# Delta rule: the decay's running sums spread from stored rows, by 16-row selector products in two row groups and two banks, two tiles at a time

## The reference, cut to what matters

```
g_cum = jnp.cumsum(g, axis=2)
diff = g_h[..., :, None] - g_h[..., None, :]
decay = jnp.where(incl, jnp.exp(jnp.where(incl, diff, 0.0)), 0.0)
l_strict = jnp.where(strict, jnp.einsum('bnthd,bnshd->bnhts', k_beta, k) * decay, 0.0)
t_inv = lax.linalg.triangular_solve(eye + l_strict, ...)
att = jnp.where(incl, jnp.einsum('bnthd,bnshd->bnhts', q, k) * decay, 0.0)
```

## Time and profile before

| | before |
|---|---|
| three runs, us | 2592.38, 2593.41, 2596.2 (median 2593.41) |
| the profiled execution's own time, us | 2584.35 |
| its span, us | 2582.4 |
| TensorE busy, us | 2280.8 (88%) |
| DVE, ACT, POOL busy, us | 965.1, 804.1, 350.5 |
| mean granted clock of TensorE | 0.934 of full speed |

### The profile page before, as it was taken

One profiled execution on the slowest core, in us unless ns is written; L12 is line 12 of the kernel. 1 busy time (PEld: TensorE's weight loads), 2 busy tenths in 40 slices (PEclk: granted clock), 3 DMA queues, 4 the chain that ended last, 5 costly groups with the idle time before them and its releaser, 6 DMA issues. The chain is left out here.

```text
span 2582.4 us, 32117 instructions
## 1 busy us (share of the span) xinstructions
PE 2280.8 (88%) x11226; PEld 1516.3 (59%) x11226; DVE 965.1 (37%) x2407; ACT 804.1 (31%) x2147; POOL 350.5 (14%) x568
## 2 busy tenths in 40 slices
PE   5999988698988878999999999989588886899998
PEld 3676555454554666555574437766375555766677
DVE  1023453555554323333331121235555553333321
ACT  2223342324333323334321112334324332334321
POOL 1000006061523000000000000000551532000000
PEclk8999999698988999999999999989788988999999
DMA  8114320221212112011221222123212222222233
GB/s 280 51 64 131 117 82 25 82 66 46 78 46 70 41 54 72 26 41 51 82 66 65 100 101 82 49 85 100 72 54 74 83 61 82 66 73 99 85 125 130
DMA packets 224617, 203.84 MB, mean 79 GB/s; under 512 B 29994, under 2 KB 219918, under 8 KB 223950
## 3 DMA queue, kind: packets, MB, share of 16 engines
q1 hardware_dynamic: 222062, 188.28, 23.3%
q0 software_dynamic: 2400, 13.52, 1.5%
HBM read 184.92 MB, written 16.85 MB: 78 GB/s over the span
## 5 line engine op out<-in xcount | busy, mean ns | idle before, releaser
L1004 PE MATMUL bank<-hT,ring 128*128 128x512 f32 (+2 forms) x1856 | 727.6, 538 | 15.9 <-ACT WORK L1514 8.1
L1004 PEld LDWEIGHTS bank<-hT,ring 128*128 128x128 f32 (+1 forms) x1856 | 337.3, 192 | 283.9 <-issue 234.5
L1004 PE MATMUL bank<-ring,hT 128*128 128x256 f32 (+2 forms) x2112 | 468.4, 377 | 37.4 <-DVE O L1725 20.3
L1004 PEld LDWEIGHTS bank<-ring,hT 128*128 128x128 f32 x2112 | 391.7, 196 | 114.4 <-issue 34.5
L1004 PE MATMUL bank<-WORK 128*128 128x128 f32 (+4 forms) x2160 | 396.9, 324 | 34.0 <-issue 15.0
L1004 PEld LDWEIGHTS bank<-WORK 128*128 128x128 f32 (+2 forms) x2160 | 306.3, 196 | 152.3 <-issue 130.3
L1004 PE MATMUL bank<-yT,ring 128*128 128x512 f32 (+1 forms) x768 | 278.3, 496 | 0.0
L1004 PEld LDWEIGHTS bank<-yT,ring 128*128 128x128 f32 x768 | 139.2, 193 | 82.8 <-issue 73.8
L971 POOL TENSOR_TENSOR WORK<-WORK 64x31 f32<-64x31 f32 (+15 forms) x248 | 150.1, 605 | 19.4
L1875 DVE SCALAR_TENSOR_TENSOR WORK<-WORK,CW 128x512 f32<-128x512 f32 (+1 forms) x192 | 147.2, 767 | 3.4
L969 POOL TENSOR_TENSOR WORK<-WORK 64x31 f32<-64x31 f32 (+15 forms) x248 | 145.6, 587 | 19.5
(11 more groups left out here) (193 smaller groups left out, 2218.4 us busy)
## 6 DMA issues: line engine op xcount, KB each, us to landing
ring<-in_w_in_dram SPq DMA_DIRECT2D x92, 1024.0 KB, 5.2
ring<-in_ada_w_dram SPq DMA_DIRECT2D x24, 1024.0 KB, 7.4
ring<-in_w_branch_dram SPq DMA_DIRECT2D x24, 1024.0 KB, 4.9
LD<-WORK SPq DMA_DIRECT2D x64, 128.0 KB, 2.0
ring<-in_w_out_dram SPq DMA_DIRECT2D x8, 1024.0 KB, 4.8
ring<-in_mla_q_up_dram SPq DMA_DIRECT2D x8, 576.0 KB, 4.6
xs<-yT POOLq DMA_DIRECT2D x2, 2048.0 KB, 9.9
O<-XD SPq DMA_DIRECT2D x32, 128.0 KB, 2.5
```

Source lines behind the costliest of these rows:

```text
L1004: return nc.tensor.matmul(o, a, b, start=start, stop=stop, skip_group_check=True)
```

## The change

Once a layer a new item `dgT` turns the running sums `GC` into rows: TensorE makes a 16x512 block (16 units x 512 tokens) twice, in output rows 64 to 79 and 96 to 111 of one bank, and ScalarE copies both into idle rows of `SLY`. A new item `d0`, for two tiles at a time, spreads one unit's row to all partitions: the weights are a column of the identity, 16 rows high, broadcast to 128 columns (a selector), the moving operand is the 16x256 block of `SLY`. Forward units read rows 64 to 79 and write the first bank of `d0`, backward units read rows 96 to 111 and write the second; the program alternates between them. `d1` loses its part on TensorE: DVE reads `d0`'s banks. Whoever takes a bank of `d0` waits for `d1` of the second of its tiles. The head's list has 16 items where it had 14.

```diff
@@ head
-        t = [[(k, l, g, tt) for k in ("d1", "d2", "dt")] for tt in range(TT)]
-        return weave(t[0], t[1]) + weave(t[2], t[3]) + [("db", l, g), ("sol", l, g)]
+        out = []
+        for p in range(2):
+            out.append(("d0", l, g, p))
+            out += [(k, l, g, 2 * p + i) for k in ("d1", "d2", "dt") for i in range(2)]
+        return out + [("db", l, g), ("sol", l, g)]
@@ gdn
-        first = [("ab", l)] + first[:4] + [("abT", l)] + first[4:10] + [("dg", l)] + first[10:]
+        first = [("ab", l)] + first[:4] + [("abT", l)] + first[4:10] + [("dg", l)] + first[10:14] + [("dgT", l)] + first[14:]
@@ NBANK
-         "dt": 0, "db": 0, "sol": 0, "xl": 0, "dv": 0, "dg": 2}
+         "d0": 2, "d1": 0, "dt": 0, "db": 0, "sol": 0, "xl": 0, "dv": 0, "dg": 2}
@@ read_at
+        if h[0] == "d0":
+            return where["d1", h[1], h[2], 2 * h[3] + 1]
@@ claim
+                elif b[0] == "d0":
+                    pe.wait_ge(*done(("d1", b[1], b[2], 2 * b[3] + 1), "dve"))
@@ tensor
-                elif k == "d1":
-                    _, l, g, tt = it
+                elif k == "dgT":
                     pe.wait_ge(*done(("dg", l), "dve"))
-                    for r in range(2):
-                        for hh in range(2):
-                            u = 2 * r + hh
-                            ins = mm(ps[:, u * P:(u + 1) * P],
-                                     col(GG, tt, g, u).broadcast_to([P, P]), kc(C_TRI + r * P))
+                    for tt in range(TT):
+                        for r in range(2):
+                            at = 64 + 32 * r
+                            ins = mm(ps[at:at + 2 * BH, tt * P:(tt + 1) * P], GC[:, tt, :], ident)
+                elif k == "d0":
+                    _, l, g, p = it
+                    pe.wait_ge(*done(("dgT", l), "act"))
+                    for hh in range(2):
+                        for r in range(2):
+                            row, at = r * BH + 2 * g + hh, 32 * r
+                            one = K[64 + at:64 + at + 2 * BH, C_ID + 64 + at + row:C_ID + 65 + at + row]
+                            ins = mm(psum(it, r)[:, hh * LC:(hh + 1) * LC], one.broadcast_to([2 * BH, P]),
+                                     SLY[64 + at:64 + at + 2 * BH, p * LC:(p + 1) * LC])
@@ scalar
+                elif k == "dgT":
+                    for at in (64, 96):
+                        ins = nc.scalar.activation(SLY[at:at + 2 * BH, 0:T], ps[at:at + 2 * BH, :], ACT.Copy)
@@ vector, d1
+                    dve.wait_ge(*done(("d0", l, g, tt // 2), "pe"))
                     for u in range(4):
                         c = slice(u * P, (u + 1) * P)
-                        ins = V_.scalar_tensor_tensor(DC[:, tt % 2, c], ps[:, c], col(GC, tt, g, u), kc(C_NEG + (u // 2) * P),
-                                                      ALU.subtract, ALU.min)
+                        c0 = u % 2 * LC + tt % 2 * P
+                        ins = V_.scalar_tensor_tensor(DC[:, tt % 2, c], psum(("d0", l, g, tt // 2), u // 2)[:, c0:c0 + P],
+                                                      col(GC, tt, g, u), kc(C_NEG + (u // 2) * P), ALU.subtract, ALU.min)
```

More of the change, by code:

```diff
@@ L314 @@
          "mkv": 2, "mq": 2, "mt": 2, "muk": 2, "muq": 2, "mkT": 2, "mqT": 2, "ms": 2, "mp": 2, "mo": 2}
-FAMILY = {"d1": "head", "d2": "head", "dt": "head", "d3": "head",
+FAMILY = {"d0": "head", "d1": "head", "d2": "head", "dt": "head", "d3": "head",
           "dv": "invert", "dx": "invert", "dya": "invert", "dyb": "invert", "dx6": "invert", "dy6": "invert",
@@ L330 @@
            "gb": ("act",), "gatt": ("dve",), "gw": ("dve",), "go": ("act", "dve"),
-           "ab": ("dve",), "abT": ("dve",), "dg": ("act", "dve"), "dqkv": ("act",), "dn": ("act",), "d1": ("dve",),
+           "ab": ("dve",), "abT": ("dve",), "dg": ("act", "dve"), "dqkv": ("act",), "dn": ("act",), "dgT": ("act",),
            "d2": ("dve",), "d3": ("act", "dve"), "dx": ("dve",), "dya": ("dve",), "dyb": ("act",), "dx6": ("act",),
@@ L661, in hybrid_block @@
         parts = {"pe": set(), "act": set(), "dve": set(), "pool": set()}
-        NOACT = {"nh", "cv", "pc", "mt", "mod", "modT", "out", "yT", "gatt", "mo", "d2", "ab", "abT",
+        NOACT = {"d0", "nh", "cv", "pc", "mt", "mod", "modT", "out", "yT", "gatt", "mo", "d2", "ab", "abT",
                  "dt", "db", "sol", "xl", "dv", "dx", "dya", "sk", "sq", "su", "sa"}
-        NODVE = {"norm", "dqkv", "pc", "dnq", "xin", "gqk", "gv", "lr", "mp", "xout", "mkT",
+        NODVE = {"d0", "dgT", "norm", "dqkv", "pc", "dnq", "xin", "gqk", "gv", "lr", "mp", "xout", "mkT",
                  "db", "sol", "xl", "dyb", "dx6", "dy6", "st"}
@@ L669, in hybrid_block @@
                 continue
-            if k not in ("nh", "cv", "dsilu", "dsil2", "dnq", "z2", "rstd", "dt", "db", "sol", "xl", "dv"):
+            if k not in ("nh", "cv", "dsilu", "dsil2", "dnq", "z2", "rstd", "d1", "dt", "db", "sol", "xl", "dv"):
                 parts["pe"].add(k)
```

## The result

| | before | after |
|---|---|---|
| median of the runs, us (4 each, same chip) | 2592.89 | 2610.59 |
| lowest and highest, us | 2592.08, 2596.2 | 2608.78, 2615.59 |
| ratio after to before, 95% interval | | 1.0074, 1.0059 to 1.0088 |
| profiled execution's own time, and span, us | 2584.35, 2582.4 | 2608.78, 2606.8 |
| mean granted clock of TensorE | 0.934 | 0.924 |

The changed kernel is slower by 0.74%, 19.2 us, where I had predicted 2.0 us faster. The last row of the table is the sum of the stretches in which the granted clock stands at half; the last such stretch reaches some 2 us beyond the span's end in every trace. The mean clock gives nearly the same: 2 x (1 - 0.924) x 2606.8 = 396.

A forecast was written before the change was run, and what follows sets the result against it. TensorE, busy for 88% of the span, was taken as the bound, with DVE pacing some heads; -2.5 - 0.4 + 0.4 + 0.5 = -2.0 us from 2593.41 gave 2591.4 us, own range 2587 to 2595, wider range 2584 to 2600.

The forecast's parts named there:

- Costs of `d0`: On TensorE in each head: row groups side by side, 0.86 us a d0 plus the change of shape; other bound 1.73.
- The change of shape: On TensorE around each d0: 0.40 us there and back between full matmuls, 0.20 behind 64x64 work; bounds 0 and 0.40.
- The step that failed: TensorE at head starts: savings counted at 2.4 GHz, 1.78 us for two tiles' d1, though they take 3.58 there.
- the forecast's prices: TensorE's saving in a head: 0.72 us in the first half and 0.52 in the second, 1.24 in all.
- `dgT`: Once a layer on TensorE, with ScalarE copies: 1.3 us, mostly covered; 0.5 us taken for both layers, bounds 0 to 2.6.
- The two more items in the head's list shift the pieces woven in by less than one piece: The head's woven list: two added items shift pieces by less than one piece; no separate time was counted.
- The new wait: Heads (0,0), (1,0): d0 for tiles 2 and 3 waits for the second tile's d1, about 1.05 us longer; +0.4 and 0.
- Rival C: Heads (0,0) and (1,0): the new wait lowers TensorE's clock, 1.8 us each, +3.6, 2595.0 us; chance 0.10.
- What the profile was to show: TensorE busy time down some 10 us or more, span down 2, wait for dv up 3 to 5 us over 66.1.

The follow-up runs named there:

- rows128: The changed kernel with sums copied to a zeroed buffer and d0's selector given 128 rows, all but one multiplying by zero; 1.0041 of before, 2599.24 us.
- both: The changed kernel with the old sixteen 128-row matmuls of a tile pair issued ahead of each d0, which overwrites them; 1.0119 of before, 2622.05 us.
- first_full: The changed kernel with d0 for tiles 0 and 1 made by the old 128-row matmuls, tiles 2 and 3 by 16 rows; 1.0046 of before, 2601.19 us.
- order_only: The changed kernel with d0 made by the old sixteen 128-row matmuls and without dgT; 1.0009 of before, 2590.91 us.
- one_group: The changed kernel with both directions of d0 read from rows 64 to 79; 1.0153 of before, 2631.53 us.

## Why the prediction was wrong

- **Costs of `d0`: right, a little high.** I took side by side, 1.26 us between full matmuls and 1.06 behind 64x64 work. Measured at 2.4 GHz: 1.06 for the second `d0` of heads (0,1) and (0,2) and 1.07 for the first of (1,0), all between full matmuls. The change of shape costs about 0.2 us there and back, half of what I read from the attention scores. Behind 64x64 work no `d0` ran at 2.4 GHz in the heads shown.
- **The step that failed:** "I count savings at 2.4 GHz, since work that moves forward into the slow stretch is slowed in their place." It takes the end of the slow stretch as given in time. It is not: the clock rose about 1 us into the old full-row work of head (0,2) and 7.2 us into the new. The account in microseconds: order 2.3 and `dgT` 4.8 are 7.1 over before, and measured is 19.2 over. If nothing of `d0`'s saving reached the end, 12 us go to the 58 us more at the lower clock; if all of it did, at the forecast's prices 8 x 1.24 = 9.9, it is 22, and at the measured 1.06 a `d0`, 16 x 0.72 = 11.5, it is 24. That is 0.2 to 0.4 for each microsecond at the lower clock, an estimate. The Trainium skill (TensorE: Matmul & The Clock Gate, Terms) puts the penalty at half the throttled time; that would be 29, an upper end here, since not all work in those stretches stands on the path that sets the time. That few-row matmuls at the start of a head are what keeps the clock low is shown by rows128, both and first_full, which bring the full rows back in three ways, and the old time of the rise with them. How many of the 19.2 us this costs is an account, not a measurement.
- **`dgT`: undersized.** "Its wait [...] is covered by the pieces of `z` and `dqkv`": that its own wait is covered says nothing of what it delays. I took 0.5, bounds 0 to 2.6; it measured 4.8. No wait of TensorE between it and the last projection in layer 1 grew shorter by it, so its 1.0 us came through; the woven piece of 1.73 and, in layer 0, a stretch of lower clock came on top. "The two more items in the head's list shift the pieces woven in by less than one piece" was said of the heads only; I did not ask it for the list into which `dgT` went.
- **The new wait: right in (0,0), too short in (1,0).** I had expected some 5 us in (0,0), 5.39 came. In (1,0) it grew by 4.2 us (4.86 to 9.09), not by about one. Together they cost little: order_only is 2.3 us over in all (0 to 4.7) against my 0.4.
- **Rival C** had the right mechanism, the lower clock, and the wrong place: a wait in two heads, at 1.8 us each. It was the absence of full matmuls, and it shows in all six heads that start in a low stretch, least in (0,1).
- **What the profile was to show:** busy time was to fall by 10 us and rose by 13.9; the wait for `dv` was to grow by 3 to 5 and grew by 1.6. The first of the two points at the clock: fewer instructions, more busy time.

Left open: what exactly of a matmul counts for the clock. With two times 64 rows side by side all 128 rows are in use and the clock rises about as early as with 128, yet its lower clock is 27 us longer; no run separates this from its `d0` being shorter. Each figure is from one profile; the seven kernels with full-row sums ahead of each tile pair (before, order_only, the three with `dgT` alone, rows128 and both) lie between 333 and 354 us, so a difference of 20 us carries weight and one of 10 doesn't. No version tried is faster than the kernel before.

## What to carry to other kernels

Before counting a saving on TensorE, ask whether the work removed is what brings the clock up; behind every wait it may be, and then what is saved on it has to be weighed against what follows at half speed. Look in a profile after for busy time that rises while instructions fall. An item inserted into a woven list costs its own time where TensorE has no wait behind it, and it can push another item ahead of a critical one; compare the order of instructions, not only their count.

## What the runs showed of the hardware

- Matmuls of 16 rows and 128 columns in two row groups and two banks run side by side, starting 7 ns apart if the program alternates and 13 ns apart if four records of one group stand first; serial they take 1.92 us for eight records at 2.4 GHz (one_group) where side by side they take 1.06, both with the change of shape.
- The granted clock comes back later when the first work behind a wait has few rows (1.2 GHz until 627.7 instead of 616.8 in head (0,2); in six heads 2.6 to 9.6 us behind DVE's first `d1` instead of -0.8 to 1.6), and stays up through the same matmuls when full ones stood ahead of them (head (0,1) of both).
- A change of the array's shape from 128 rows to 16 and back cost 0.2 us (1.06 against 4 x 0.216 = 0.86).
